# Loading each expert matrix of a fused two-block kernel as two transfers instead of one

## The chip, the core and the metric

The kernel runs on one core of one Trainium2 chip. A core has five engines with their own instruction streams: TensorE (matmuls into PSUM, in the rows PE, its weight loads PEld), VectorE (DVE), ScalarE (ACT), GpSimd (POOL) and SyncE (SP), which here only issues transfers between DRAM and SBUF. The core's 16 DMA engines carry these out. The metric is the device time of one execution in microseconds; lower is better. The rows speak of the granted clock of TensorE (PEclk): 1.00 is its full level of 2.4 GHz, and a mean below 1 says that for a part of the stretch it ran at 1.2 GHz.

## What is computed

Two blocks of a language model run one after another on 256 tokens of width 1024, in float32. The first has two layers of three attention branches and a feed-forward part; the second has one layer with dilated attention, an RWKV-7 mixer and a mixture of experts. The change touches the mixture of experts alone. Its constants, and what its last part has to compute (cut from the reference, names of helpers shortened):

```python
N_EXPERT_GROUPS = 4
EXPERTS_PER_GROUP = 8
N_EXPERTS = N_EXPERT_GROUPS * EXPERTS_PER_GROUP
TOP_K = 2
D_EXPERT = 512
```

```
h      = rms_norm(x)                                   # 256 x 1024
group  = argmax over 4 of softmax(h @ w_group_router)
e1, e2 = the best two of the group's 8 experts, with gates g1, g2
y[row] = sum over e in (e1, e2) of
         g_e * ((silu(h[row] @ w_gate[e]) * (h[row] @ w_up[e])) @ w_down[e])
x      = x + y
```

Each of the 32 experts has three matrices: gate and up, 1024 x 512, and down, 512 x 1024. Each is 2.097 MB, so that 96 matrices with 201 MB are read.

## The kernel before

The program is written with explicit semaphores, one instruction stream for each engine. The first block and most of the second run until about 1255 us of the span; the last quarter is the expert stage.

**The loop over experts.** A turn handles two experts (`EPT` = 2), 64 rows of tokens for each, side by side in one 128-wide tile. 16 turns (`TURNS`) handle all 32 experts; further passes would follow only if more than 64 tokens chose one expert, which they don't here. The loop over `body` has two turns in one pass (`h` = 0, 1), and its first pass starts with turn 0.

**What TensorE does in a turn** (from L1420 on): the gate matmuls of both experts, then the up matmuls (both L1425), the gathering of the rows for the next turn (L1392), four transposes (L1434), the giving back of the last turn's result (L1401), four more transposes (L1443), and the down matmuls (L1451). ScalarE and VectorE apply silu, product and gate between these.

**The slots.** There is room for the matrices of one turn: six slots `moe_slot[0..5]` of 16 KB in each partition, two for gate (0, 1), two for up (2, 3), two for down (4, 5). The first four lie in the tile `ring`, the last two in `arena`. The host has laid the matrices out so that a partition's 4096 numbers stand together in DRAM, and one transfer fills one slot: 128 rows of 16 KB.

**Who loads when.** SP issues all these transfers on one queue, in the order gate, up, down for a turn. `next_matrices` (L892) issues a pair when TensorE has finished reading the pair's slots in the turn before (`read.wait_full`): the next gate pair when the gate matmuls of this turn are done, the next up pair when the up matmuls are done, the next down pair when the last down matmul is done. The matrices of turn 0 are loaded earlier, by L884, while the block's last projections still run.

**Who waits for them.** Each slot has a semaphore `moe_loaded[s]`, which a transfer raises by 16 when it has landed. `arrived` (L1415) makes TensorE wait for both slots of a pair before it starts the pair's matmuls. In a pass of the loop each slot is filled twice, hence 32 for a pass and 16 for each `h`.

Of the kernel before, what the change touches and what calls it, by code (L numbers as in the profile page):

```python
# [69 lines left out]
SLOT = 4096  # L70
# [347 lines left out]
EPT = 2  # L418
# [89 lines left out]
def program(nc, io, out):  # L508
    tables = shape_tables()
    with ExitStack() as ctx:  # L510
# [3 lines left out]
        def sem(name):  # L514
            return ctx.enter_context(nc.semaphore(name))
# [61 lines left out]
        def area(o, n):  # L577
            return arena1[:, o:o + n]
# [79 lines left out]
        moe_slot = [ring[:, s * SLOT:(s + 1) * SLOT] for s in range(SLOTS)] + [area(j * SLOT, SLOT) for j in range(2)]  # L658
# [96 lines left out]
        moe_loaded = [sem(f"moe_loaded{s}") for s in range(MOE_SLOTS)]  # L755
# [11 lines left out]
        def second_weight(name):  # L767
            kind, b = name
            if kind == "att_out":
                return io["w_att_out_2"][0].rearrange("(k p) n -> p k n", p=P), HPG * ATT_E // P, D  # L770
            if kind == "rwkv_out":
                return io["w_rwkv_out_2"][0].rearrange("(k p) n -> p k n", p=P), RW_W // P, D
            return io["w_out_2"][0, :, b * 512:b * 512 + 512].rearrange("(k p) n -> p k n", p=P), KD, 512

        def second_piece(name):
            kind, b, i = name
            first_col = {"qkv": 0, "rw": 3 * ATT_W, "gate": 3 * ATT_W + RW_IN}[kind]
            c, w = {"rw": RW_BLOCKS, "qkv": QKV_BLOCKS, "gate": GATE_BLOCKS}[kind][b]
            src = io["w_in_2"][0, i * 256:(i + 1) * 256, first_col + c:first_col + c + w]
            return src.rearrange("(k p) n -> p k n", p=P), 2, w  # L780
# [8 lines left out]
        def layer_weight(name, l):  # L789

            kind, b, i = name
            if kind == "in":
                c, w = IN_BLOCKS[b]
                src = io["w_in"][l, i * 512:(i + 1) * 512, c:c + w]
            elif kind == "uq":
                src, w = io["w_uq"][l, i * 2 * P:(i + 1) * 2 * P, :], MLA_H * QK
            elif kind == "ukv":
                src, w = io["w_ukv"][l], MLA_H * (NOPE + MLA_V)
            elif kind == "out":
                src, w = io["w_out"][l, i * 512:(i + 1) * 512, b * 512:(b + 1) * 512], 512  # L800
            elif kind == "ff1":
                src, w = io["w_ff1"][l, :, b * 512 + i * 256:b * 512 + (i + 1) * 256], 256
            else:
                src, w = io["w_ff2"][l, b * 512 + i * 256:b * 512 + (i + 1) * 256, :], D
            k = {"in": 4, "uq": 2, "ukv": KV_RANK // P, "out": 4, "ff1": KD, "ff2": 2}[kind]
            return src.rearrange("(k p) n -> p k n", p=P), k, w
# [18 lines left out]
        def _(sp):  # L825
# [3 lines left out]
            with sp.Fori(0, DEPTH) as l:  # L829
                for j, (name, _, _) in enumerate(LW.pieces):  # L830
                    LW.wait_raw_free(sp, j, l)
                    src, k, w = layer_weight(name, l)
# [5 lines left out]
            for j, (name, _, _) in enumerate(PW.pieces):  # L838
                PW.wait_raw_free(sp, j, 0)
                src, k, w = second_piece(name)  # L840
# [29 lines left out]
            for name, _ in SW.blocks:  # L870
                s = SW.where[name][0]
                src, k, w = second_weight(name)
                sp.dma_start(slot(s, k * w).rearrange("p (k n) -> p k n", k=k), src).then_inc(slot_loaded[s], 16)

            def matrices(first_expert):

                for i, w in enumerate(("w_expert_gate_2", "w_expert_up_2", "w_expert_down_2")):
                    for j in range(EPT):
                        yield moe_slot[EPT * i + j], io[w][first_expert + j], EPT * i + j

            for dst, src, s in matrices(0):

                units.wait_full(SW.last[s] if s < SLOTS else ("oT", 1))
                sp.dma_start(dst, src).then_inc(moe_loaded[s], 16)  # L884
            sp.wait_ge(places_ready, 1)

            def next_matrices(first_expert, read, half):

                for dst, src, s in matrices(first_expert):
                    if s % EPT == 0:  # L890
                        read.wait_full((("gate", half), ("up", half), ("y", half, 1))[s // EPT])
                    sp.dma_start(dst, src).then_inc(moe_loaded[s], 16)  # L892
# [36 lines left out]
        def _(pe):  # L929
# [42 lines left out]
            with pe.Fori(0, DEPTH) as l:  # L972
# [34 lines left out]
                w = MLA_H * QK // 2  # L1007
# [36 lines left out]
                for t in range(T):  # L1044
                    bank = units.begin(("retO", t))
                    for h in range(RET_H):
                        mine = [i for i, u in enumerate(RET_UNITS) if (u[0], u[2]) == (t, h % 2)]
                        for i in mine:
                            s = RET_UNITS[i][1]
# [92 lines left out]
            def weights(name):  # L1142
                s, i = SW.where[name]
                pe.wait_ge(slot_loaded[s], 16 * i)
                return second_slot(name)
# [106 lines left out]
            w = weights(("att_out", 0))  # L1252
# [6 lines left out]
            for t in range(T):  # L1259
# [43 lines left out]
                for par in range(2):  # L1303
# [3 lines left out]
                    for c in range(PAIRS):  # L1307
                        o = bank[:, c * RW_E:(c + 1) * RW_E]
# [11 lines left out]
                for par in range(2):  # L1320
# [3 lines left out]
                    for c in range(PAIRS):  # L1324
                        o = bank[:, c * RW_E:(c + 1) * RW_E]
# [5 lines left out]
                if t == 0:  # L1331
                    bank = units.begin(("state", 0))
                    for c in range(PAIRS):
                        o, cols = bank[:, c * P:(c + 1) * P], slice(c * P, (c + 1) * P)
# [13 lines left out]
            w = weights(("rwkv_out", 0))  # L1348
# [8 lines left out]
            for c in range(2):  # L1357
                w = weights(("out", c))
# [28 lines left out]
            def gather(i, par):  # L1387

                for kk in range(4):
                    k = 4 * i + kk  # L1390
                    for t in range(T):
                        ins = pe.matmul(psum[:, 6 + i, kk * P:(kk + 1) * P], xn2[:, t, k * P:(k + 1) * P],  # L1392
                                        take[par][:, t, :, :].rearrange("p j n -> p (j n)"), start=(t == 0), stop=(t == T - 1))
                return ins

            def give_back():

                for u in range(2 * T):
                    t, c = u // 2, u % 2
                    for part in range(2):  # L1400
                        pe.matmul(final.bank(("acc", u)), takeT[:, t * P:(t + 1) * P], y_parts[:, part, c * 512:(c + 1) * 512],  # L1401
                                  start=False, stop=False)
# [8 lines left out]
            with pe.Fori(0, bodies) as body:  # L1411
                units = RoundView(EU, pe, psum, body)

                def arrived(s, k, h):
                    pe.wait_ge(moe_loaded[s], body * 32 + (16 * h + 16))  # L1415
                    return moe_slot[s].rearrange("p (k n) -> p k n", k=k)

                for h in range(2):
                    units.wait_emptied(("gx", 1 - h, 1), 1 - h)
                    for i, stage in enumerate(("gate", "up")):  # L1420
                        w = [arrived(EPT * i + j, KD, h) for j in range(EPT)]
                        bank = units.begin((stage, h))
                        for k in range(KD):
                            for j in range(EPT):
                                ins = pe.matmul(bank[half(j), :], xe[h][:, k, half(j)], w[j][:, k, :], start=(k == 0), stop=(k == KD - 1))  # L1425
                        units.finish((stage, h), ins)
                    pe.wait_ge(take_ready, body * 2 + (2 + h))
                    for i in range(2):
                        units.begin(("gx", h, i))
                        units.finish(("gx", h, i), gather(i, 1 - h))  # L1430
                    units.wait_emptied(("up", h))
                    bank = units.begin(("hT", h))
                    for f in range(D_EXP // P):
                        ins = pe.transpose(bank[:, f * P:(f + 1) * P], hid[:, f * P:(f + 1) * P], ident)  # L1434
                    units.finish(("hT", h), ins)

                    units.wait_emptied(("gt", 1 - h), 1 - h)
                    units.wait_emptied(("y", 1 - h, 1), 1 - h)
                    give_back()
                    bank = units.begin(("gt", h))  # L1440
                    for i, a in enumerate((give[h], take[h])):
                        for t in range(T):
                            ins = pe.transpose(bank[:, i * SEQ + t * P:i * SEQ + (t + 1) * P], a[:, t, :, :].rearrange("p j n -> p (j n)"), ident)  # L1443
                    units.finish(("gt", h), ins)
                    w = [arrived(2 * EPT + j, D_EXP // P, h) for j in range(EPT)]
                    units.wait_emptied(("hT", h))
                    for c in range(2):
                        bank = units.begin(("y", h, c))
                        for f in range(D_EXP // P):
                            for j in range(EPT):  # L1450
                                ins = pe.matmul(bank[half(j), :], hidT[:, f, half(j)], w[j][:, f, c * 512:(c + 1) * 512],  # L1451
                                                start=(f == 0), stop=(f == D_EXP // P - 1))
                        units.finish(("y", h, c), ins)
# [1035 lines left out]
```

## Time and profile before

| | us |
|---|---|
| median of three runs | 1745.15 |
| lowest and highest of them | 1742.68 and 1747.34 |
| the profiled execution, its own time | 1741.68 |
| its span, first to last instruction | 1739.9 |
| TensorE busy (matmuls) | 1595.0 |
| VectorE, ScalarE, GpSimd busy | 687.0, 518.9, 518.7 |

All rows come from one profiled execution, and times in them count from the start of its span. Outside the span lie 1.8 us. The expert stage has its first gate matmul at 1264.28 and its last down matmul ends at 1727.55; give-back, final sums and the store of the output follow. Busy shares are averages: for a stage that two engines share, the list of waits and the chain that ended last tell which of them the other waits for.

### The profile page before, as it was taken

How to read it: one execution, taken by the hardware profiler on the slowest of the kernel's cores; microseconds unless marked ns; L12 is line 12 of the kernel's file. 1: busy time of each engine (PE TensorE's matmuls, PEld its weight loads, DVE VectorE, ACT ScalarE, POOL GpSimd, SP SyncE). 2: the span in 40 equal slices, each digit the busy share in tenths (PEclk: the TensorE clock that was granted, in tenths of full speed). 3: DMA queues.
4: the chain of work that ended last, by engine and by line, in shares of the span. 5: the costliest groups of instructions: out<-in, count | busy, mean ns of one | idle time of the engine just before them, and what ended most of it. 6: DMA issues, size and time to landing. Idle time of an engine off the chain costs nothing.

```text
span 1739.9 us, 22256 instructions
## 1 busy us (share of the span) xinstructions
PE 1595.0 (92%) x8598; PEld 1182.1 (68%) x8598; DVE 687.0 (39%) x1103; ACT 518.9 (30%) x707; POOL 518.7 (30%) x195
## 2 busy tenths in 40 slices
PE   7976999999967899999898998999899999999998
PEld 6865889997857789998676767985545343434343
DVE  1187355554067636554331845532312121111112
ACT  4335243344334334333443442110201111111111
POOL 5744324443845234432687802100000000000000
PEclk9978699999978699999898999979899999999999
DMA  6422145553532025554576341001479999999994
GB/s 212 149 73 70 30 142 193 184 182 121 164 126 73 25 97 170 194 194 158 164 213 211 100 179 53 1 1 49 193 305 428 429 428 428 429 429 428 429 428 203
DMA packets 97282, 351.78 MB, mean 202 GB/s; under 512 B 5059, under 2 KB 43887, under 8 KB 84655
## 3 DMA queue, kind: packets, MB, share of 16 engines
q1 hardware_dynamic: 96510, 349.35, 53.7%
q8 instruction: 55, 0.90, 0.2%
q10 hardware_dynamic: 576, 1.12, 0.2%
q0 software_dynamic: 112, 0.17, 0.1%
q14 instruction: 29, 0.24, 0.0%
HBM read 347.70 MB, written 1.07 MB: 200 GB/s over the span
## 4 chain that ended last, share of the span: by engine, by line
PE 40%; issue 23%; DMA 15%; POOL 14%; DVE 4%; POOLq 2%; ACT 2%; SPq 0%; DVEq 0%; ACTq 0%
DMA ring<-in_w_expert_up 14%; POOL weights_split L816 11%; PE psum L1425 9%; PE psum L935 6%; PE psum L937 6%; PE psum L936 6%; PE psum L925 3%; PE psum L1451 2%; PE psum L1392 1%; POOLq L1771 1%; POOL arena L1822 1%; PE psum L1294 1%; PE psum L1401 1%; DMA arena<-arena 1%; PE psum L907 1%
## 5 line engine op out<-in xcount | busy, mean ns | idle before, releaser
L816 POOL TENSOR_TENSOR weights_split<-weights_raw,weights_split 128x2048 fp32r<-128x2048 f32 (+5 forms) x124 | 450.0, 3642 | 426.0 <-ACT weights_split L1520 425.8
L1520 ACT ACTIVATE weights_split<-weights_raw 128x2048 fp32r<-128x2048 f32 (+5 forms) x156 | 243.7, 1565 | 336.0 <-PE psum L937 334.6
L1425 PE MATMUL psum<-ring,arena 128*64 128x512 f32 x1024 | 228.8, 601 | 22.0 <-DMA ring<-in_w_expert_up 20.9
L935 PE MATMUL psum<-weights_split,h_split 128*128 128x512 f32 (+4 forms) x528 | 200.4, 380 | 11.3 <-DVE arena L2120 6.8
L937 PE MATMUL psum<-weights_split,h_split 128*128 128x512 f32 (+4 forms) x528 | 198.8, 377 | 0.0
L936 PE MATMUL psum<-weights_split,h_split 128*128 128x512 f32 (+4 forms) x528 | 198.6, 376 | 0.0
L1425 PEld LDWEIGHTS psum<-ring,arena 128*64 128x64 f32 x1024 | 74.3, 138 | 173.2 <-issue 173.2
L935 PE MATMUL psum<-h_split,weights_split 128*128 128x256 f32 x512 | 145.0, 283 | 0.9 <-DVE h_split L1508 0.9
L937 PE MATMUL psum<-h_split,weights_split 128*128 128x256 f32 x512 | 144.9, 283 | 0.0
L936 PE MATMUL psum<-h_split,weights_split 128*128 128x256 f32 x512 | 144.9, 283 | 0.0
L935 PEld LDWEIGHTS psum<-weights_split,h_split 128*128 128x128 f32 x528 | 101.3, 192 | 32.9 <-issue 13.0
L1451 PE MATMUL psum<-arena 128*64 128x512 f32 x512 | 113.4, 595 | 0.0
L936 PEld LDWEIGHTS psum<-weights_split,h_split 128*128 128x128 f32 x528 | 101.2, 192 | 16.8
L937 PEld LDWEIGHTS psum<-weights_split,h_split 128*128 128x128 f32 x528 | 101.0, 191 | 17.1
L935 PE MATMUL psum<-weights_split,hidden_split 128*128 128x512 f32 x256 | 99.8, 390 | 0.0
L936 PE MATMUL psum<-weights_split,hidden_split 128*128 128x512 f32 x256 | 99.8, 390 | 0.0
L935 PEld LDWEIGHTS psum<-h_split,weights_split 128*128 128x128 f32 x512 | 98.2, 192 | 2.1 <-POOL weights_split L816 1.7
L937 PE MATMUL psum<-weights_split,hidden_split 128*128 128x512 f32 x256 | 99.6, 389 | 0.0
L936 PEld LDWEIGHTS psum<-h_split,weights_split 128*128 128x128 f32 x512 | 98.2, 192 | 0.5
L937 PEld LDWEIGHTS psum<-h_split,weights_split 128*128 128x128 f32 x512 | 98.2, 192 | 0.0
L907 PE MATMUL psum<-shared_c 128*128 128x256 f32 x348 | 84.8, 403 | 10.2 <-DMA phase_c<-in_first_c 8.1
L2061 DVE TENSOR_TENSOR hidden_split<-arena,hidden_split 128x512 fp32r<-128x512 f32 x32 | 86.1, 2691 | 15.8 <-ACT hidden_split L1617 15.8
(339 smaller groups left out, 2149.7 us busy)
## 6 DMA issues: line engine op xcount, KB each, us to landing
weights_raw<-in_w_ff SPq DMA_DIRECT2D x64, 1024.0 KB, 5.4
ring<-in_w_expert_gate SPq DMA_DIRECT2D x32, 2048.0 KB, 16.1
ring<-in_w_expert_up SPq DMA_DIRECT2D x32, 2048.0 KB, 17.1
arena<-in_w_expert_down SPq DMA_DIRECT2D x32, 2048.0 KB, 13.4
weights_raw<-in_w_in SPq DMA_DIRECT2D x44, 512.0 KB, 4.5
weights_raw<-in_w_in SPq DMA_DIRECT2D x20, 1024.0 KB, 5.2
weights_raw<-in_w_out SPq DMA_DIRECT2D x8, 1024.0 KB, 5.1
weights_raw<-in_w_uq SPq DMA_DIRECT2D x6, 768.0 KB, 4.5
```

The source lines that it names most:

```text
L816: eng.tensor_tensor(W.part(j, 1, n), W.raw(j, n), W.part(j, 0, n).bitcast(F32), ALU.subtract).then_inc(W.lo[W.pieces[j][1]], 1)
L907: pe.matmul(bank[:, 0:SEQ], ident, shared("causal")[:, 0:SEQ], start=True, stop=True)
L925: ins = pe.matmul(bank[:, 0:n], lhs(i), w[:, i, :], start=(i == 0), stop=(i == k - 1))
L935: pe.matmul(out, a[0], b[0], start=first, stop=False)
L936: pe.matmul(out, a[0], b[1], start=False, stop=False)
L937: return pe.matmul(out, a[1], b[0], start=False, stop=last)
L1294: ins = pe.matmul(bank[:, c * P:(c + 1) * P], m[left_m][:, c, :], m[right_m][:, c, :], start=True, stop=True)
L1392: ins = pe.matmul(psum[:, 6 + i, kk * P:(kk + 1) * P], xn2[:, t, k * P:(k + 1) * P], take[par][:, t, :, :].rearrange("p j n -> p (j n)"), ...
L1425: ins = pe.matmul(bank[half(j), :], xe[h][:, k, half(j)], w[j][:, k, :], start=(k == 0), stop=(k == KD - 1))
L1451: ins = pe.matmul(bank[half(j), :], hidT[:, f, half(j)], w[j][:, f, c * 512:(c + 1) * 512], start=(f == 0), stop=(f == D_EXP // P - 1))
L1520: act.activation(W.part(j, 0, w), W.raw(j, w), ACT.Copy).then_inc(W.hi, 1)
L2061: dve.tensor_tensor(part[1], hid_sq[i % 4], part[0].bitcast(F32), ALU.subtract).then_inc(hid_ready.sem, 1)
```

## The change

Each of the 96 matrices is loaded by two transfers, one for the first 2048 numbers (8 KB) of every partition and one for the second. Both go to the slot in which the whole went, and both raise the slot's semaphore by 16. The wait in `arrived` asks for twice the count, 64 for a pass and 32 for each `h`, so that both halves have landed before a matmul reads the slot. Bytes, slots, order of the matrices and all other instructions stay.

```diff
                 for i, w in enumerate(("w_expert_gate_2", "w_expert_up_2", "w_expert_down_2")):
                     for j in range(EPT):
-                        yield moe_slot[EPT * i + j], io[w][first_expert + j], EPT * i + j
+                        for o in range(0, SLOT, SLOT // 2):
+                            yield moe_slot[EPT * i + j][:, o:o + SLOT // 2], io[w][first_expert + j, :, o:o + SLOT // 2], EPT * i + j
...
                 def arrived(s, k, h):
-                    pe.wait_ge(moe_loaded[s], body * 32 + (16 * h + 16))
+                    pe.wait_ge(moe_loaded[s], body * 64 + (32 * h + 32))
                     return moe_slot[s].rearrange("p (k n) -> p k n", k=k)
```

On SP, in the loop over the turns, one turn's loads stood like this before (`ring` holds the gate and up slots, `arena` the down slots; the number behind a name is the shape of one transfer in numbers of float32, and the name in brackets the semaphore on which the row waits):

```order
L892 ISA [waits moe_unit_full]
L892 DMA ring<-in_w_expert_gate 128x4096
L892 ISA
L892 DMA ring<-in_w_expert_gate 128x4096
L195 REGISTER_ALU
L892 DMA ring<-in_w_expert_up 128x4096 [waits moe_unit_full]
L892 DMA ring<-in_w_expert_up 128x4096
L195 REGISTER_ALU
L892 DMA arena<-in_w_expert_down 128x4096 [waits moe_unit_full]
L892 DMA arena<-in_w_expert_down 128x4096
```

and in the changed kernel, from the second expert's gate matrix on:

```order
L893 ISA
L893 DMA ring<-in_w_expert_gate 128x2048
L893 ISA
L893 DMA ring<-in_w_expert_gate 128x2048
L195 REGISTER_ALU
L893 DMA ring<-in_w_expert_up 128x2048 [waits moe_unit_full] x2
L893 DMA ring<-in_w_expert_up 128x2048 x2
L195 REGISTER_ALU
L893 DMA arena<-in_w_expert_down 128x2048 [waits moe_unit_full] x2
L893 DMA arena<-in_w_expert_down 128x2048 x2
```

There are twelve transfers in a turn where there were six, of half the width and in the same order of matrices; of each pair's four, the two halves of the first matrix wait on the semaphore, as its one transfer did. No row moved past another, and on the other engines nothing but a constant of TensorE's waits changed.

## Rows read from the trace of the kernel before

**Rows 1.** The page: span, and lines of the 40 slices (43.5 us each).

```profile
span 1739.9 us, 22256 instructions
...
PE   7976999999967899999898998999899999999998
...
DMA  6422145553532025554576341001479999999994
GB/s 212 149 73 70 30 142 193 184 182 121 164 126 73 25 97 170 194 194 158 164 213 211 100 179 53 1 1 49 193 305 428 429 428 428 429 429 428 429 428 203
```

**Rows 2.** Waits of TensorE between 1264 and 1735 us: total, times, longest.

```profile
PE psum L1425 <- DMA ring<-in_w_expert_up: 20.9, 13, 1.9
PE psum L1401 <- DVE y_parts L2449: 1.6, 1, 1.6
PE psum L1425 <- DVEq L2430: 1.1, 1, 1.1
```

**Rows 3.** The chain that ended last, 1320 to 1370 us: start, us, what.

```profile
1333.20 21.11 DMA ring<-in_w_expert_up
1354.30 0.23 issue
1354.53 7.11 PE psum L1425 x32
...
1362.08 21.59 DMA ring<-in_w_expert_up
```

**Rows 4.** The same chain in the last two turns.

```profile
1677.55 8.78 PE psum L1425 x32
...
1699.85 6.87 PE psum L1425 x32
1706.72 0.20 issue
1706.92 7.09 PE psum L1425 x32
1714.01 3.77 PE psum L1392 x32
1717.77 0.44 PE psum L1434 x4
1718.21 1.86 PE psum L1401 x8
1720.07 0.44 PE psum L1443 x4
1720.51 7.04 PE psum L1451 x32
```

**Rows 5.** Windows: length, busy of five engines, PEclk, DMA share, GB/s.

```profile
1383.90:1413.30 29.40, 29.20 (x146) 13.19 (x146) 5.37 (x15) 3.01 (x7) 0.00 (x0) 0.94 1.01 429
1677.50:1706.90 29.40, 29.16 (x144) 13.15 (x144) 5.35 (x15) 2.97 (x7) 0.00 (x0) 0.94 1.01 428
1354.50:1706.90 352.40, 332.91 (x1728) 153.51 (x1728) 65.19 (x180) 48.40 (x90) 0.00 (x0) 0.99 1.01 428
```

**Rows 6.** SP's transfers in order of time: start, us for the pair, line, what.

```profile
1271.45 0.80 SPq L892 DMA_DIRECT2D ring<-in_w_expert_gate  x2
1278.27 0.80 SPq L892 DMA_DIRECT2D ring<-in_w_expert_up  x2
1291.78 1.01 SPq L892 DMA_DIRECT2D arena<-in_w_expert_down  x2
```

**Rows 7.** Windows again: 4 KB rows, 2 KB rows, and around the hole.

```profile
1008.00:1013.00 5.00, 4.50 (x26) 3.08 (x25) 2.15 (x6) 3.42 (x8) 0.00 (x0) 1.00 1.02 420
1015.00:1023.00 8.00, 8.00 (x41) 5.11 (x40) 2.53 (x8) 3.15 (x10) 0.00 (x0) 1.00 1.05 387
1275.00:1285.00 10.00, 10.00 (x66) 7.03 (x64) 2.07 (x3) 0.83 (x2) 0.00 (x0) 1.00 1.02 437
1293.00:1297.00 4.00, 4.00 (x22) 1.30 (x19) 2.05 (x11) 0.00 (x0) 0.00 (x0) 1.00 0.91 352
1297.00:1301.00 4.00, 4.00 (x20) 1.29 (x18) 0.00 (x0) 0.60 (x1) 0.00 (x0) 1.00 1.01 430
```

**Rows 8.** A lone transfer's landing (page), and L873's issues, min/median/max in ns.

```profile
xs<-in_x SPq DMA_DIRECT2D x1, 1024.0 KB, 4.9
...
L873 SPq DMA_DIRECT2D ring<-in_w_out x2: 508/2760/5011, 1005.0 to 1005.5; - x2
```

## The prediction

> **What bounds the kernel now.** I read the slices of the page first. In the last quarter of the span, from about 1300 us, the DMA row stands at 9 and the rate at 428 to 429 GB/s in every slice, while TensorE is 9 tenths busy too [rows 1]. Two engines that are both full say little, so the second view is the list of waits on TensorE in the expert stage. It names one large releaser: the expert matmuls wait 20.9 us in 13 waits for the transfer of an `up` matrix [rows 2]. No other wait there is over 2 us. The third view is the chain that ended last. It runs through this stage as one repeated pattern: the end of the `up` matmuls of a turn frees the two `up` slots, SP issues two transfers, 21.6 us later they have landed, TensorE multiplies for 7.11 us and frees the slots again [rows 3]. From one start of the `up` matmuls to the next it is always 29.37 us: from 1354.53 [rows 3] to 1706.92 [rows 4] are 352.39 us for 12 turns.
>
> The 21.6 us are not a latency that could be shortened by itself. A turn loads six matrices (two experts, three matrices each), so a matrix takes 352.39 / 72 = **4.894 us**, and the windows show a DMA share of 1.01 at 428 GB/s over exactly this stretch [rows 5]: 2.097 MB / 4.894 us is the same 428.5 GB/s. TensorE's own work in a turn is less. In the last turn, which hardly waits, the gate matmuls take 6.87 us and all that follows them up to the end of the down matmuls 20.6 us, together 27.5 us [rows 4]. So in each turn some 1.9 us of TensorE's time wait for the queue. The stage is bound by the DMA stream, which stands in one queue that never runs empty, and TensorE follows it.
>
> From where on is the stream unbroken? SP's rows give the issue times: the `down` matrices for turn 1 at 1291.78, then gate, up, down for each later turn [rows 6]. In the 4 us around 1295 the DMA share is 0.91, before it a full window, and after it 1.01 [rows 7]. So there is one short hole, between the last `up` of turn 1 and the `down` matrices that TensorE released late, and none afterwards. Behind that hole come 2 `down` matrices for turn 1, six matrices for each of the turns 2 to 14, and gate and up of turn 15, whose landing releases the last wait: 2 + 13 x 6 + 4 = **84 matrices**. As a cross-check, 84 x 4.894 = 411.1 us before 1706.7 is 1295.6, where the hole is.
>
> **The change, part by part.** (1) *Bytes.* The same 201 MB go to the same slots, and a wait of TensorE still asks for both halves of both matrices (64 in place of 32 per pass of the loop). So no matmul can start on half a matrix, and the change cannot bring the arrival forward.
>
> (2) *Rows.* A transfer puts a row into each of 128 partitions; with 16 DMA engines each moves 8 rows per matrix now, of 16 KB, and 16 rows of 8 KB after it, so 8 more per matrix and engine. What does a row cost beyond its bytes? The trace before has no saturated stretch with 8 KB rows, so I bound it by its neighbours. With 4 KB rows (32 per matrix and engine), the load of `w_rwkv_out`, the engines were full at 420 GB/s; with 2 KB rows (64), the two of `w_out`, at 387 GB/s [rows 7]. In time for 2.097 MB: 4.894 us with 8 rows, 4.993 with 32, 5.419 with 64. That is 0.099 / 24 = 4.1 ns per added row by the one, 0.525 / 56 = 9.4 ns by the other. For 8 more rows: **33 ns** or **75 ns** per matrix. I take 75. By size of row the 4 KB stretch is nearer, but by kind the 2 KB one is: `w_out` is loaded as column halves, so that each read takes a half of a source row and leaves the other, as the changed transfers do, while `w_rwkv_out` is read in whole rows, one after another. Both ends stay for the range.
>
> (3) *Transfers.* There are six more per turn, each with its own completion. In rows of before this can't be told apart from the rows' cost: the 4 KB and the 2 KB stretches consist of transfers as large as those of the experts. I bound it from below by nothing and from above by one more row of the dearer kind, 9 ns per matrix.
>
> (4) *SP.* Now it issues two transfers in some 0.8 us [rows 6], afterwards four in 1.6 us. Twelve issues of 0.4 us are 4.9 of the 29.4 us of a turn. The transfers behind them are covered: those of `up` land 21.6 us after they are issued, of which the pair itself needs 9.8, so that almost 12 us of earlier transfers stand in front of them. Cost: nothing. Only at 1271.45 and at 1291.78, where the queue is empty or nearly so, is there no cover, and there the first half still goes out at the same moment as the whole did. The two halves each wait on the count that the whole waited on, and it has been reached by then.
>
> (5) *Sum.* 84 x 0.075 = **6.3 us**, with ends 84 x 0.033 = 2.8 and 84 x 0.084 = 7.1. All of it is on the path: the landing of the last `up` matrices moves from 1706.7 to 1713.0, and behind it stands the same work of TensorE, VectorE and the output as before. The slower stream before the hole (four matrices, 0.3 us) fills a piece of the hole. The two `down` matrices behind the last `up` would land 0.15 us later still, against about 4 us of slack: 9.8 us of loading against 13.6 us from 1706.92 to their use at 1720.51 [rows 4].
>
> What TensorE does meanwhile changes little. In two turns its granted clock fell to a mean of 0.94 [rows 5], that is, for a part of the turn it ran at the lower of its two levels, 1.2 GHz instead of 2.4; the `up` matmuls took 8.78 us instead of 7.11 there [rows 4], each time after it had waited for the queue. The 1.7 us vanished in the 1.9 us of waiting, and with the changed kernel there are 2.3. Only a fall behind the last landing, in the last 20.7 us, would show in the time: some 20.7 / 29.4 of a turn, where now 2 turns of 12 have one, so about one chance in ten, at 1.7 us.
>
> **What the skill says against it.** The rows show a cost per row between 4.1 and 9.4 ns [rows 7]. The Trainium skill, "DMA: Bandwidth & Descriptors", section "Why small descriptors are slow (HBM only)", gives a fixed overhead of about three cycles per packet inside the DMA engine on trn2. With that page's 850 MHz this is an estimate of 3.5 ns, near the lower of my ends, and by it the sum would be 84 x 8 x 3.5 ns = 2.4 us. And "SBUF — State Buffer", section "The DMA setup-cost knee", has every transfer pay roughly 2 us and advises one DMA, not several; paid one after another, 84 more transfers would be an estimated 168 us.
>
> **Rivals.** *A: the short price, no measurable change.* If a row costs 4.1 ns, the time is 1745.15 + 2.8 = 1747.9. For it: 4 KB rows are nearer in size, and there the share was 1.02 at 420 GB/s. Against it: the 2 KB rows show that a cut source row can cost more. It decides below 62 ns per matrix (84 x 62 ns is 5.2 us, 0.3% of the time, about what a measurement of this kernel can tell from no change). Chance 0.33.
>
> *B: each transfer pays its latency.* A single transfer of 1024 KB (the load of `x`) lands 4.9 us after its issue [rows 8], where its bytes need 2.45, so 2.45 us are latency. If the queue paid that for each transfer, 84 more would add 206 us: 1951. Against it: then a matrix would now take 4.9 + 2.45 = 7.3 us, and they come every 4.894. It would need a queue that holds only few transfers: the issue of a `w_out` matrix did stretch from 0.4 to 5.0 us [rows 8], with 64 rows per engine each and others ahead; but the engines stayed full then (1.05) [rows 7]. Chance 0.02.
>
> *C, the other side: shorter rows stream better.* If an engine overlaps the end of one row with the start of the next, and more boundaries help, the rate could rise to what it was for the first matrices after a pause, 437 GB/s between 1275 and 1285 [rows 7]. Then a matrix takes 4.80 us, a turn 28.8, still above the 27.5 of TensorE, and 84 x 0.095 = 8.0 us are saved: 1737.2. It decides as soon as the changed stream goes above 429 GB/s. Against it: from 16 to 4 to 2 KB the rate only falls. Chance 0.05.
>
> **How the numbers follow.** Forecast (75 ns): 0.60. A: 0.33. B: 0.02. C: 0.05. The profiled execution took 1741.68 us (span 1739.9), so the forecast for it is 1748.0. The median of the three runs is 3.5 us above it, since the runs scatter over 1742.68 to 1747.34; the change is added to the median: **1751.4 us**. Range: the forecast and A with the ends 2.8 and 7.1 give 1747.9 to 1752.3; a clock fall at the end adds 1.7, and the median of a few runs scatters by some 1.3 either way: 1746.5 to 1755.0. Chances: slower by over 0.3% 0.60 (most of the forecast, and B), within 0.3% 0.35 (A, and the part of the forecast that the scatter of the runs pulls below 5.2 us), faster 0.05 (C).
>
> **What would show it.** In the changed profile the windows of turns 3 to 14 should keep a DMA share of 1.00 or more at a lower rate, 428.5 x 4.894 / 4.969 = 422 GB/s (A: 425.6; C: above 429); the `up` matmuls should start every 29.8 us (A: 29.57); TensorE's wait for the `up` transfers should grow from 20.9 us by about 6; and the packets of the queue should rise by 96 x 128 = 12,288 of data. Nothing before 1290 us should move. If the DMA share falls below 1 in those windows, step 4 was wrong and SP or the queue's depth has become the bound; if the rate falls and the time does not, the path is not where I see it.

## The result, and the profile after

| | before | changed |
|---|---|---|
| median of eight runs, us | 1744.12 | 1751.49 |
| lowest and highest, us | 1740.94 and 1749.23 | 1749.39 and 1754.21 |
| profiled execution, us (span) | 1741.68 (1739.9) | 1753.39 (1751.6) |

The ratio is **1.004, with a 95% interval of 1.0026 to 1.0055**: slower by 0.4%, or between 4.5 and 9.6 us. The page of the changed kernel shows the expert stage in the slices from about 1310 us on. Span, the DMA row, the rate and the count of packets answer to [rows 1]; the issues of the expert matrices stand under them (transfers, KB each, median us from issue to landing):

```profile
span 1751.6 us, 22464 instructions
...
DMA  6422145553432035555476341001489999999994
GB/s 211 147 72 72 31 144 192 188 185 117 154 124 72 26 97 169 193 192 165 155 211 210 108 169 53 1 1 58 183 337 422 422 422 422 422 422 422 422 422 201
DMA packets 111106, 351.79 MB, mean 201 GB/s; under 512 B 6595, under 2 KB 45423, under 8 KB 86191
...
ring<-in_w_expert_gate SPq DMA_DIRECT2D x64, 1024.0 KB, 16.2
ring<-in_w_expert_up SPq DMA_DIRECT2D x64, 1024.0 KB, 17.1
arena<-in_w_expert_down SPq DMA_DIRECT2D x64, 1024.0 KB, 13.5
```

The engines are as full as before and carry less: 422 GB/s where it was 428 and 429. The packets under 512 B rose from the 5059 of the page before to 6595: 1,536, which is 16 for each of the 96 added transfers. Packets of at least 8 KB (the difference of the first and the last count) rose from 12,627 to 24,915, by 12,288 = 96 x 128 rows. So the change did what it says: twice the rows, twice the transfers, the same bytes.

TensorE's waits in the stage answer to [rows 2]:

```profile
PE psum L1426 <- DMA ring<-in_w_expert_up: 25.9, 14, 2.4
PE psum L1402 <- DVE y_parts L2450: 1.6, 1, 1.6
PE psum L1426 <- DVEq L2431: 1.1, 1, 1.1
```

The one large wait grew from 20.9 to 25.9 us. It has one stop more, 14 instead of 13, because turn 2 now waits for its `up` matrices too; no other releaser joined it. The chain that ended last has the same pattern as [rows 3] and [rows 4], here at turn 3 and at the last two turns:

```profile
1339.42 21.06 DMA ring<-in_w_expert_up
1360.48 0.23 issue
1360.72 7.11 PE psum L1426 x32
...
1658.96 8.80 PE psum L1426 x32
...
1688.79 7.11 PE psum L1426 x32
...
1718.60 7.09 PE psum L1426 x32
1725.68 3.77 PE psum L1393 x32
...
1732.18 7.04 PE psum L1452 x32
```

From the `up` matmuls of turn 3 to those of turn 15 are 1718.60 - 1360.72 = 357.88 us, so a turn takes 29.82 us and a matrix **4.971 us**, against 4.894 before. The window over just this stretch, to be held against [rows 5] (same columns):

```profile
1360.70:1718.60 357.90, 334.63 (x1729) 153.86 (x1729) 65.13 (x180) 48.81 (x90) 0.00 (x0) 0.99 1.01 422
```

**Where the time went.** The two profiled spans differ by 11.7 us, more than the medians. SP's rows split this (they answer to [rows 6]):

```profile
1276.18 1.94 SPq L893 DMA_DIRECT2D ring<-in_w_expert_gate  x4
...
1296.52 2.78 SPq L893 DMA_DIRECT2D arena<-in_w_expert_down  x4
```

The first transfer of the stage's loop is issued at 1276.18 instead of 1271.45, so 4.7 us of the difference lie before it. They are older than anything that the change touches: SP issues the first expert transfer of all, a gate matrix for turn 0, at 1069.07 instead of 1064.39, and the load of `w_rwkv_out` before it at 1008.57 instead of 1004.00. In the experiments below the start of the loop lies between 1270.7 and 1275.6, in kernels with one, two or four transfers for each matrix alike: it is scatter of the earlier part. From there to the last `up` matmuls are 442.42 us against 435.47, **6.95 us more**. All of it comes after the `down` issues for turn 1 (422.08 us against 415.14), behind the hole. What follows the last `up` matmuls is the same as before, to 0.1 us.

### The profile page after: what moved, and what is told of

It reads as the page before. It is cut to its first block, busy times and chain, and to the rows that moved or that the text cites. A ratio compares the mean times of both kernels' runs of the same rounds, so it can differ in the third digit from the quotient of the medians.

```text
span 1751.6 us, 22464 instructions
## 1 busy us (share of the span) xinstructions
PE 1601.9 (91%) x8598; PEld 1186.2 (68%) x8598; DVE 686.9 (39%) x1103; ACT 519.0 (30%) x707; POOL 518.5 (30%) x195
## 2 busy tenths in 40 slices
DMA packets 111106, 351.79 MB, mean 201 GB/s; under 512 B 6595, under 2 KB 45423, under 8 KB 86191
## 4 chain that ended last, share of the span: by engine, by line
PE 37%; issue 23%; DMA 18%; POOL 14%; DVE 4%; POOLq 2%; ACT 2%; SPq 1%; DVEq 0%; ACTq 0%
DMA ring<-in_w_expert_up 16%; POOL weights_split L816 11%; PE psum L1426 8%; PE psum L936 6%; PE psum L937 6%; PE psum L938 6%; PE psum L926 3%; POOLq L1772 1%; POOL arena L1823 1%; SPq L893 1%; PE psum L1452 1%; PE psum L1393 1%; PE psum L1295 1%; DMA arena<-arena 1%; PE psum L908 1%
## 5 line engine op out<-in xcount | busy, mean ns | idle before, releaser
L1426 PE MATMUL psum<-ring,arena 128*64 128x512 f32 x1024 | 230.6, 604 | 27.0 <-DMA ring<-in_w_expert_up 25.9
```

## The experiments

Two theories for the 76 ns per matrix were open. R: a row costs a fixed time beyond its bytes. T: a transfer does. The change doubled both, so that its own profile can't tell them apart. In all runs a turn is read off the chain as above, from turn 3 to turn 15, and divided by six matrices. "Rows for each matrix and engine" are the 128 rows of a matrix divided by 16 engines, or a multiple of that. The before kernel ran beside each on the same chip; the ratios are to it.

### Rows without transfers

```diff
-                        yield moe_slot[EPT * i + j], io[w][first_expert + j], EPT * i + j
+                        yield (moe_slot[EPT * i + j].rearrange("p (o n) -> p o n", o=2),
+                               io[w][first_expert + j].rearrange("o p n -> p o n"), EPT * i + j)
...
-        arrays[name] = np.ascontiguousarray(w.reshape(NE, -1, P, w.shape[2]).transpose(0, 2, 1, 3).reshape(NE, P, SLOT))
+        arrays[name] = np.ascontiguousarray(w.reshape(NE, -1, P, w.shape[2]).transpose(0, 2, 1, 3).reshape(NE, P, 2, SLOT // 2).transpose(0, 2, 1, 3))
```

> One transfer for each matrix as before, but in rows of 8 KB: the matrix lies in DRAM as two blocks of 128 x 8 KB, and the transfer takes both. Rows as in the changed kernel, transfers as in the kernel before. Theory R (each row costs some 9.5 ns beyond its bytes): 8 more rows per matrix and engine, 4.97 us for a matrix, 29.82 us for a turn, +6 to +7 us in all. Theory T (each transfer costs 76 ns, a row nothing): 4.894 us, a turn of 29.37 us, no change. Half and half would be a turn of 29.6 us.

Measured: 1752.06 us, ratio 1.0046 (1.0033 to 1.006). The `up` matmuls of turn 3 and turn 15 stand in the chain at

```profile
1354.93 7.11 PE psum L1426 x32
...
1712.73 7.09 PE psum L1426 x32
```

that is 357.80 us for 12 turns, 4.969 us for a matrix: the whole loss of the change, with one transfer for each matrix. R holds, T falls.

The same with four blocks instead of two:

> One transfer for each matrix in rows of 4 KB (four blocks of 128 x 4 KB in DRAM): 24 more rows per matrix and engine than before. Theory R with 9.5 ns a row: 5.12 us for a matrix, a turn of 30.73 us, +19 us. R with the 4.1 ns of the 4 KB rows of w_rwkv_out: a matrix 4.99 us, a turn of 29.96 us, +8 us. Theory T: no change.

Measured: 1766.69 us, ratio 1.0126 (1.0104 to 1.0149). The same two starts in its chain:

```profile
1360.60 8.61 PE psum L1426 x32
...
1729.24 8.59 PE psum L1426 x32
```

and a window of its expert stage:

```profile
1400.00:1700.00 300.00, 274.95 (x1404) 125.32 (x1404) 53.60 (x149) 40.67 (x75) 0.00 (x0) 0.97 1.03 410
```

368.64 us for 12 turns, 5.120 us for a matrix, and full engines at 410 GB/s. The expected 5.12 of the dearer price came out; the 4.99 of the cheaper one did not, although the rows are 4 KB and whole. Then with eight blocks:

> One transfer for each matrix in rows of 2 KB (eight blocks of 128 x 2 KB in DRAM): 56 more rows per matrix and engine than before. With 9.4 ns a row: 4.894 + 0.526 = 5.42 us for a matrix (387 GB/s, as the loads of w_out), a turn of 32.5 us, 84 x 0.526 = +44 us or some more, as the hole is filled. If the price rises for small rows, more than that.

Measured: 1792.59 us, ratio 1.0265 (1.0236 to 1.0295). The `up` matmuls of turn 15 start 390.32 us after those of turn 3, 5.421 us for a matrix. The price stays the same down to rows of 2 KB.

### Transfers without rows

> Two transfers for each matrix, split by partitions (0 to 63 and 64 to 127), with rows of 16 KB as before. Transfers as in the changed kernel, rows as before. Theory R: a turn of 29.37 us, no change. Theory T: 29.82 us, +6 to +7 us. If 64 partitions don't load all DMA engines and ports alike, the rate falls far more than either says (a turn over 31 us), and the run tells nothing on R and T but shows that.

```diff
-                        yield moe_slot[EPT * i + j], io[w][first_expert + j], EPT * i + j
+                        for o in range(0, P, P // 2):
+                            yield moe_slot[EPT * i + j][o:o + P // 2, :], io[w][first_expert + j, o:o + P // 2, :], EPT * i + j
```

(TensorE's wait asks for the doubled count, as in the changed kernel.) Measured: 2186.2 us, ratio 1.2524 (1.2494 to 1.2555). In the stage:

```profile
1400.00:1700.00 300.00, 175.00 (x732) 74.46 (x730) 27.06 (x75) 19.71 (x37) 0.00 (x0) 0.76 1.01 212
```

The DMA share is full and the rate is half, 212 GB/s. So this run tells nothing on R and T, as its expectation allowed; what it shows is told at the end. The question was put again from the other side, with half the transfers and the same rows:

```diff
-                    for j in range(EPT):
-                        yield moe_slot[EPT * i + j], io[w][first_expert + j], EPT * i + j
+                    yield (moe_pair[i].rearrange("p (j n) -> p j n", j=EPT),
+                           io[w][bass.ds(first_expert, EPT)].rearrange("j p n -> p j n"), EPT * i)
```

(`moe_pair[i]` are the two neighbouring slots of a pair. Both now fill with one transfer, so TensorE waits on one semaphore for the pair; these lines are left out here.)

> One transfer for the two matrices of a pair, rows of 16 KB as before: rows as before, half the transfers. Theory R (rows only): 4.894 us for a matrix, a turn of 29.37 us, no change. If a transfer's end costs its own few ns on each engine (at most 9 ns, the duration of the completion packet): 4.890 us, a turn of 29.34 us, -0.4 us.

Measured: 1745.56 us, ratio 1.001 (0.9997 to 1.0022). The starts of `up` in turns 3 and 15 are 1354.85 and 1707.26: 352.41 us, 4.895 us for a matrix, as before. And with four transfers for each matrix (and four times the count in TensorE's wait), whose rows are those of the one-transfer run with 4 KB:

> The change once more: four transfers of 4 KB for each partition and matrix. It has the rows of the run with one transfer of 4 KB rows and four times its transfers. Theory R (9.4 ns a row, nothing for a transfer): 5.12 us for a matrix, a turn of 30.72 us, +19 us as there plus what the later start costs. Rival: SP's 24 issues of a turn (some 11 of 30.7 us) or the completions come through: more than 5.15 us for a matrix, or a DMA share below 1.

Measured: 1765.17 us, ratio 1.0111 (1.0084 to 1.0137). The starts are 1359.62 and 1728.29: 5.120 us for a matrix, the same as with a quarter of the transfers. SP's rows from the stage:

```profile
1418.03 8.52 SPq L893 DMA_DIRECT2D ring<-in_w_expert_gate  x8
1429.91 6.89 SPq L893 DMA_DIRECT2D ring<-in_w_expert_up  x8
```

Eight issues take 8.5 us here instead of 8 x 0.4, so an issue can stretch; yet the window from 1400 to 1700 has a DMA share of 1.03, and the stream does not slow. A transfer of 0.5 to 4 MB, with its issue and its completion, costs nothing that these runs can tell from zero while others stand in front of it.

### The reason given for the price

The prediction took 75 ns because the changed kernel reads half rows of its source. This run leaves all of the change in and takes that away; the host lays the matrices out in two blocks, as in the run with one transfer and 8 KB rows:

```diff
-                        for o in range(0, SLOT, SLOT // 2):
-                            yield moe_slot[EPT * i + j][:, o:o + SLOT // 2], io[w][first_expert + j, :, o:o + SLOT // 2], EPT * i + j
+                        for o in range(2):
+                            yield (moe_slot[EPT * i + j][:, o * (SLOT // 2):(o + 1) * (SLOT // 2)],
+                                   io[w][first_expert + j, o], EPT * i + j)
```

> As the changed kernel (two transfers of 8 KB rows for each matrix), but each half of a matrix lies in DRAM as a block of its own, so that no transfer leaves a half of a source row out. The prediction took the dearer price for a row because the changed kernel's reads are such cut rows (theory C). C: the price falls to 4.1 ns a row, 4.93 us for a matrix, a turn of 29.6 us, half of the loss. Theory R (the row's price does not depend on where the rest of the source row lies): 4.97 us for a matrix, a turn of 29.82 us, as the changed kernel.

Measured: 1751.03 us, ratio 1.0047 (1.0027 to 1.0068). The starts are 1359.09 and 1717.04: 4.972 us for a matrix. The theory C of the expectation falls: whether the other half of the source row stands right behind the half that is read does not matter.

### Is the stream the only path?

These two kernels load the down matrices for turn 0 alone, and all later turns multiply by those, so their output is not that of the model. The stream has a third less to carry. The lines are those of the kernel with whole matrices; the one with halves has 32 in place of 16 and the doubled counts.

```diff
                 for dst, src, s in matrices(first_expert):
+                    if s >= 2 * EPT:
+                        continue
...
-                    pe.wait_ge(moe_loaded[s], body * 32 + (16 * h + 16))
+                    pe.wait_ge(moe_loaded[s], 16 if s >= 2 * EPT else body * 32 + (16 * h + 16))
```

> The kernel before, with the down matrices loaded for turn 0 alone; all later turns use those. Loading takes 4 x 4.89 = 19.6 us of a turn, so the stage should be bound by TensorE: turns of 27.2 to 27.3 us, no wait for an up matrix, some 1718 us in all. It is the base for nodown_split.

> The changed kernel with the same left out: down matrices loaded for turn 0 alone. If the loss of the change is the stream's rate and nothing else (the theory), it is gone here: the same time as nodown_whole within 0.1%, turns of 27.2 to 27.3 us. Rival: a part of the loss is SP's doubled issues or the landing of the second half: then it stays here, +2 us or more against nodown_whole.

Measured: 1718.62 us with whole matrices, 1715.32 us with halves. The gate and up matmuls stand in the two chains (first the kernel with whole matrices, turns 1 and 15) at

```profile
1295.06 13.73 PE psum L1427 x64
...
1676.51 13.73 PE psum L1427 x64
```

and with halves

```profile
1291.27 13.73 PE psum L1428 x64
...
1672.72 13.73 PE psum L1428 x64
```

Both take 381.45 us for 14 turns, 27.25 us each. In neither does TensorE wait for an `up` matrix. The 3.3 us between the medians are not in the stage: the profiled spans, 1716.1 and 1712.3, differ by 3.8 us, and so does the first of these rows, 1295.06 against 1291.27. So where loading is not what bounds the stage, the split costs nothing: the loss needs the full stream. In that full stream SP's issues and the landing of a second part were still a possible cost; the runs with equal rows and one, two and four transfers exclude that.

### The other direction

If rows cost, fewer and longer ones gain. Here the two matrices of a pair lie in DRAM so that each partition's 32 KB stand together, and one transfer loads them:

```diff
-                    for j in range(EPT):
-                        yield moe_slot[EPT * i + j], io[w][first_expert + j], EPT * i + j
+                    yield moe_pair[i], io[w][first_expert // EPT], EPT * i
```

> The other way: one transfer for the two matrices of a pair, which lie in DRAM so that a partition's 32 KB stand together. 4 rows fewer per matrix and engine, half the transfers. Theory R: 38 ns less per matrix, a turn of 29.14 us, -3.2 us. Theory T gives the same here (half a transfer fewer per matrix). If a row of 32 KB is cut by the hardware into pieces of 16 KB or less, R says no change.

Measured: 1741.65 us, ratio 0.999 (0.9974 to 1.0007).

> The kernel with one transfer for a pair in rows of 32 KB, again and with more rounds, since its first interval of the ratio (0.9974 to 1.0007) held no change. By its profile a matrix takes 4.857 us instead of 4.894, so the stage should gain 84 x 0.037 = 3.1 us: a ratio of 0.998.

Measured: 1742.35 us against 1746.59 us of the before kernel beside it, ratio **0.9979 (0.9963 to 0.9995)**. The two starts in the chain of the first run:

```profile
1355.84 7.11 PE psum L1426 x32
...
1705.56 7.09 PE psum L1426 x32
```

and the window of its expert stage:

```profile
1400.00:1700.00 300.00, 283.18 (x1483) 130.13 (x1480) 57.16 (x161) 42.05 (x77) 0.00 (x0) 1.00 1.00 432
```

349.72 us for 12 turns, 4.857 us for a matrix, 432 GB/s. The two ratios are one gain of 0.1 to 0.2%, small beside the scatter of the runs; the first interval alone doesn't exclude no change, the second does. It is the fastest kernel of this study that computes everything. Theory T expected the same gain here, but half the transfers with 16 KB rows gave none, so it comes from the rows. A row of 32 KB is moved as one packet: the page counts 90,369 packets, 6,144 = 96 x 64 fewer than the 96,513 of that run.

### All rows together

| bytes of a row | rows per matrix and engine | us for a matrix |
|---|---|---|
| 32 KB | 4 | 4.857 |
| 16 KB (before; half the transfers) | 8 | 4.894; 4.895 |
| 8 KB (one; two transfers; two of whole blocks) | 16 | 4.969; 4.971; 4.972 |
| 4 KB (one; four transfers) | 32 | 5.120; 5.120 |
| 2 KB | 64 | 5.421 |

From the first to the last line are 0.564 us for 60 rows, **9.4 ns a row**, and each step between gives 9.2 to 9.5 (with the mean of each line). Carried on to no row at all, which no run has, this is an estimate of 4.857 - 4 x 0.0094 = 4.819 us, 435 GB/s.

## Why the prediction was right, and where not

**What bounds.** Held. The stage is bound by one unbroken stream; with a third of it gone, the change costs nothing. TensorE's own turn, put at 27.5 us, is 27.25 there.

**The count of 84 matrices.** Held to half a microsecond. 84 x 0.076 = 6.4 us of the measured 6.95, and turns 4 to 15 lost what they should, 5.5 us; the rest sits in the first matrices behind the hole. The prediction let the hole swallow the 0.3 us of the four matrices before it. It seems to have swallowed only a part. From the `down` issues for turn 1 to the last `up` matmuls the kernels with 8 KB rows took 6.94 (changed), 6.57 (one transfer) and 6.50 us (whole blocks) more than before, those with 4 KB rows 19.63 and 19.08, the one with 2 KB rows 45.66. At their own prices for a matrix (0.075 to 0.077, 0.226 and 0.527 us) these are 84 to 91 matrices, where 84 were counted and 88 would be with the four. Why the changed kernel lies at the upper end is open; its four issues behind the hole took 2.78 us, where the two before took 1.01, and no run was made on that.

**The price of a row.** The number held (75 ns forecast, 76 measured: 5.49 us in 72 matrices), **the reason did not**. The choice between 33 and 75 ns was made on the ground that cut source rows are dearer, and the run with whole blocks took that ground away. Of the two rows that gave the ends [rows 7], the one of `w_rwkv_out` misled: it was read in the first nine microseconds after a pause. The run with one transfer and 4 KB rows has the same in small: 419 GB/s from 1300 to 1305 us, right behind its hole, and 410 from 1318 on and in all the rest. The `w_out` row stood behind it in the same queue, and its 387 GB/s came out again in the run with 2 KB rows. So 9.4 ns was the better of the two prices for another reason than the one given, and that the forecast came out rests in part on luck. The better ground for choosing, in this trace, was which row lies deeper in an unbroken stream.

**Transfers and SP.** Held. No charge for a transfer, and doubled and even fourfold issues stay covered. The prediction named beside this a fixed time for each transfer (the Trainium skill, "SBUF — State Buffer", section "The DMA setup-cost knee"). For transfers that queue behind others the trace does not agree: half as many gave 4.895 us for a matrix, the same. The other rule that it named, three cycles a packet (the Trainium skill, "DMA: Bandwidth & Descriptors", section "Why small descriptors are slow (HBM only)"), is an estimate of 3.5 ns, less than half of the measured 9.4 ns.

**The rivals.** A needed a price below 62 ns a matrix and got 76. B and C are excluded: a matrix came every 4.971 us, not every 7.3 or 4.80, with a share of 1.01 at 422 GB/s. C's rate of 437 was that of one window and too high, as told at the end.

**The signs named beforehand.** Rate 422 GB/s forecast and measured; a turn of 29.8 us forecast and 29.82 measured; the wait was to grow by about 6 us and grew by 5.0, because three turns had the slower clock (`up` matmuls of 8.8 us) instead of two, and a slow turn waits less (1.7 us). None fell behind the last landing. The 12,288 added data packets came out. One sign failed: nothing before 1290 us was to move, and 4.7 us had been lost there, before the first expert transfer. Without it the profiled execution would lie 7 us above the one before.

**The sum.** 6.3 us were forecast; the stage of the profiled execution lost 6.95, and the medians of eight runs differ by 7.4, inside the interval of 4.5 to 9.6 us. The forecast of 1751.4 us meets the measured 1751.49 better than the parts deserve: it was built on a median of three runs that lies 1.0 us above that of eight.

## What to carry to other kernels

Where full DMA engines bound a stage, count the rows that each engine moves and multiply by a price per row read from a long stream in the same trace; the number of transfers did not enter here, from 0.5 to 4 MB each, as long as others stood ahead of them in the queue. Splitting a load can pay only where something can start on the first part, and here nothing could; a kernel that starts on the first half was not tried. Before laying out weights, ask whether what is loaded together can stand together in a partition.

## What the runs showed of the hardware

**A stream is a little faster just after a pause, and a short window makes it look like more.** With 4 KB rows the difference is 2%: `w_rwkv_out` moved at 420 GB/s [rows 7] and the long stream of such rows at 410. With 16 KB rows [rows 7] has 437 against 428 [rows 5]. But the rate of a window counts each packet whole where it starts, and the 16 engines' packets of 16 KB start nearly together after a pause (stretches of 2 us of the burst below read 401 to 467); one round of them is 262 KB, which is 26 GB/s in 10 us. Moved by 1 us either way, the window 1275 to 1285 of before reads 426 and 428. With the down matrices left out each turn has a pause; this window is of that kernel, with whole matrices and rows of 16 KB:

```profile
1391.00:1400.00 9.00, 9.00 (x60) 6.45 (x60) 1.76 (x3) 1.45 (x4) 0.00 (x0) 1.00 1.02 437
```

Its neighbours 1 us away read 428 and 430, and the whole stretch from 1387 to 1404 reads 432. So with 16 KB rows some 431 to 433 GB/s after a pause stand against 428 later, 1% at most. What makes the difference, the time, the number of rows since the pause or how many transfers stand in the queue, was not tried.

**64 partitions at a time halve the rate.** A transfer to partitions 0 to 63 and one to 64 to 127, one behind the other, ran at 212 GB/s with a DMA share of 1.01, instead of 428. The Trainium skill, "SBUF — State Buffer", section "Door 1: The DMA port swizzle (why `[64,N]` ≈ `[32,N]`)", says that partitions 0 to 63 reach only half of the DMA ports of SBUF; the run agrees, though it shows the rate and not the ports.

**More waiting, slower clock, no cost.** TensorE's granted clock in the window from 1400 to 1700 us is 0.97 with 4 KB rows, where the `up` matmuls take 8.6 us in every second turn, against 0.99 before, where it was two turns of twelve. Each slow turn there comes right after a wait of 3.3 us for the queue, and the queue covers it: the turns stay at 30.72 us.
